# Two seven-product down-projections of a streaming-encoder trunk: their first four products interleaved instead of half after half

## What is computed

```python
for i in range(DEPTH):                      # DEPTH = 4
    h = _rmsnorm(x, norm_mix[i])
    ...                                     # y = mixer of this layer
    x = x + y
    x = x + jnp.square(jax.nn.relu(_rmsnorm(x, norm_mlp[i]) @ mlp_w1[i])) @ mlp_w2[i]
return _rmsnorm(x, norm_final)              # mlp_w1: 1024 x 4096, mlp_w2: 4096 x 1024
```

## Time and profile before

| what | value |
|---|---|
| median of three runs | 2018.82 us |
| the profiled execution: its own time | 2018.45 us |
| the profiled execution: first to last instruction | 2016.7 us |
| granted TensorE clock over the span | 0.999 of full speed |
| TensorE / VectorE / ScalarE / GpSimd busy | 98% / 78% / 55% / 17% |
| share of the chain that ended last | TensorE 84%, VectorE 11%, ScalarE 3% |
| eight stretches from the first down product of slice 1 or 2 to the next up product | 360.61 us, 45.05 or 45.12 each |

### The profile page before, as it was taken

The page is one execution under the profiler, slowest core; times in us unless marked ns, Lnnn a source line. Parts: engine busy times, 40 slices in busy tenths (PEclk is TensorE's granted clock), DMA queues, the critical chain, the costliest instruction groups (busy, mean ns, idle before and its releaser), DMA issues.

```text
span 2016.7 us, 31611 instructions
## 1 busy us (share of the span) xinstructions
PE 1975.1 (98%) x12912; PEld 1779.3 (88%) x12912; DVE 1572.5 (78%) x1898; ACT 1100.7 (55%) x1540; POOL 346.7 (17%) x403
## 2 busy tenths in 40 slices
PE   9999999999999999999999999999999999999998
PEld 7888899999878889999888889999988888899997
DVE  7866878885898878887598786888687758688874
ACT  6655534545466645455456663554647646354463
POOL 7002001110200201113731201111731011011100
PEclk9999999999999999999999999999999999999999
DMA  6122457765222266667332145685632123468761
GB/s 192 63 67 72 140 136 167 194 141 162 89 85 91 87 157 157 159 155 184 119 88 71 58 151 139 165 205 141 169 86 71 57 69 126 110 166 189 173 189 42
DMA packets 232352, 256.31 MB, mean 127 GB/s; under 512 B 19632, under 2 KB 191216, under 8 KB 232208
## 3 DMA queue, kind: packets, MB, share of 16 engines
q1 hardware_dynamic: 183024, 207.01, 32.2%
q0 software_dynamic: 46784, 45.89, 14.6%
q10 hardware_dynamic: 2400, 1.38, 0.2%
HBM read 248.21 MB, written 2.10 MB: 124 GB/s over the span
## 4 chain that ended last, share of the span: by engine, by line
PE 84%; DVE 11%; ACT 3%; issue 2%; DMA 0%; SPq 0%; DVEq 0%; ACTq 0%
PE psum L772 26%; PE psum L774 25%; PE psum L773 25%; DVE w_lo L1611 2%; PE psum L1245 2%; DVE u_lo L1844 1%; ACT w_hi L2663 1%; DVE arena_r L1844 1%; DVE x L1901 1%; PE psum L1218 1%; DVE arena L1850 1%; PE psum L1353 1%; DVE h_lo L1638 1%; PE psum L1194 1%; PE psum L1190 1%
## 5 line engine op out<-in xcount | busy, mean ns | idle before, releaser
L1611 DVE TENSOR_TENSOR w_lo<-w_raw,w_hi 128x1024 fp32r<-128x1024 f32 x339 | 415.1, 1232 | 193.7 <-ACT w_hi L2663 192.3
L2663 ACT ACTIVATE w_hi<-w_raw 128x1024 fp32r<-128x1024 f32 x343 | 358.4, 1058 | 367.3 <-PE psum L774 237.4
L772 PE MATMUL psum<-u_hi,w_hi 128*128 128x512 f32 (+1 forms) x1256 | 439.9, 350 | 12.0 <-DVE u_lo L1844 7.4
L772 PE MATMUL psum<-h_hi,w_hi 128*128 128x256 f32 (+1 forms) x1368 | 440.6, 322 | 1.1 <-DVE w_lo L1611 1.1
L773 PE MATMUL psum<-h_lo,w_hi 128*128 128x256 f32 (+1 forms) x1368 | 437.3, 320 | 0.0
L774 PE MATMUL psum<-h_hi,w_lo 128*128 128x256 f32 (+1 forms) x1368 | 437.3, 320 | 0.0
L774 PE MATMUL psum<-u_hi,w_lo 128*128 128x512 f32 (+1 forms) x1256 | 433.9, 345 | 0.0
L773 PE MATMUL psum<-u_lo,w_hi 128*128 128x512 f32 (+1 forms) x1128 | 398.4, 353 | 0.0
L773 PE MATMUL psum<-arena_r,w_hi 128*128 128x256 f32 x1184 | 331.8, 280 | 0.0
L772 PEld LDWEIGHTS psum<-h_hi,w_hi 128*128 128x128 f32 x1368 | 260.1, 190 | 21.1 <-DVE w_lo L1611 1.6
L773 PEld LDWEIGHTS psum<-h_lo,w_hi 128*128 128x128 f32 x1368 | 260.4, 190 | 19.1 <-issue 1.2
(11 more groups left out here) (380 smaller groups left out, 3208.0 us busy)
## 6 DMA issues: line engine op xcount, KB each, us to landing
w_raw<-in_mlp_w SPq DMA_DIRECT2D x204, 512.0 KB, 4.9
arena<-in_mlp_w SPq DMA_DIRECT2D x92, 512.0 KB, 4.9
w_raw<-in_mlp_w POOLq DMA_DIRECT2D x52, 512.0 KB, 6.1
arena<-in_mlp_w POOLq DMA_DIRECT2D x28, 512.0 KB, 6.0
w_raw<-in_mla_w_o SPq DMA_DIRECT2D x16, 512.0 KB, 3.5
w_raw<-in_lru_w_in SPq DMA_DIRECT2D x16, 512.0 KB, 4.0
w_raw<-in_swa_w_in SPq DMA_DIRECT2D x12, 512.0 KB, 3.9
w_raw<-in_mla_w_ukv SPq DMA_DIRECT2D x8, 512.0 KB, 4.2
```

The lines of the kernel that those rows point to most:

```text
L772: nc.tensor.matmul(out, stat[0], mov[0], start=start, stop=False, skip_group_check=skip)
L1611: ins = nc.vector.tensor_tensor(w_lo[:, to], tile, exact(w_hi[:, to]), ALU.subtract)
L2663: nc.scalar.activation(w_hi[:, to], raw_tile(op.raw), ACT.Copy).then_inc(w_hi_done, 1)
```

## The change

The two `seven_down` become one `both_down`. TensorE runs `U11` for half 0 and half 1, then `UT1` for both, `U21` for both, `UT3` for both; then `UT2`, `UT4`, `U22` of half 0, and the same three of half 1. The number of products, matmuls, loads, accumulating DMAs, splits and additions is as before; only the order is new, on all five engines. The weights' order follows (`raws` and `ops` in the plan), and so do DVE's and ACT's streams. A11+A21 is now given up before the last sum instead of after it, so its slot comes free one tile earlier. The diff, cut to the functions that stand in the new order:

```diff
@@ -200,28 +200,34 @@ (weight_plan)
-    def seven_down(i, s, g):
...
+    def both_down(i, s):
+        def blocks(g):
+            return blocks_of(lambda half, n: ("w2_block", i, s * SLICE + half * T, g * T + n, BLOCK))
+        halves = blocks(0), blocks(1)
+        for order in (0, 4, 2, 3, 1):
+            raws.extend(half[order] for half in halves)
+        for a, e, b, p, q in halves:
+            ops.append(Operand("A11", a))
+            a.freed = len(ops)
+        for a, e, b, p, q in halves:
+            ops.append(Operand("A21+A22", q))
+            q.freed = len(ops)
+        for a, e, b, p, q in halves:
+            ops.append(Operand("A12", b))
+        for a, e, b, p, q in halves:
+            ops.append(Operand("A11+A21", p, (p, e)))
+        for g, (a, e, b, p, q) in enumerate(halves):
+            ops.append(Operand("A11+A21+A22", p, made=sums + 1 + g))
+            down_sums.append((b, p))
+            ops.append(Operand("A22", e))
+            p.freed = e.freed = len(ops)
+            ops.append(Operand("A11+A12+A21+A22", b, made=sums + 3 + g))
+            b.freed = len(ops)
+        sums += 4
...
-        raws.extend((a, q, b, p, e))
...
@@ -298,6 +304,7 @@
+X_FIRST, X_V, X_Y, X_Z, X_SECOND = (1, 2), (3, 5), (7, 8), (9, 10), (11, 13)
@@ -951,32 +958,35 @@ (tensor engine)
-            def seven_down(g):
...
+            def both_down():
+                c.add("downs", 2)
+                halves = (0, 1), (2, 3)
+                for g, (xy, own) in enumerate(halves):
+                    claim(xy)
+                    pe.wait_ge(u_turned, n + 1)
+                    group(bank(xy, 0), U11, False)
+                for g, (xy, own) in enumerate(halves):
+                    claim(own)
+                    pe.wait_ge(u_turned, n + 2)
+                    group(bank(own, 1), UT1, False)
+                for g, (xy, own) in enumerate(halves):
+                    pe.wait_ge(u_turned, n + 3)
+                    group(bank(xy, 1), U21, False)
+                for g, (xy, own) in enumerate(halves):
+                    pe.wait_ge(u_turned, n + 4)
+                    group(bank(own, 0), UT3, False)
+                for g, (xy, own) in enumerate(halves):
+                    pe.wait_ge(u_turned, n + 5)
+                    pe.wait_ge(x_added, 7 * d + X_FIRST[g])
+                    group(bank(xy, 0), UT2, True)
+                    pe.wait_ge(u_turned, n + 7)
+                    pe.wait_ge(x_added, 7 * d + X_Z[g])
+                    group(bank(own, 0), UT4, True)
+                    pe.wait_ge(x_added, 7 * d + X_SECOND[g] + 1)
+                    group(bank(xy, 0), U22, True)
@@ -1887,60 +1896,91 @@ (vector engine)
-            def seven_down(g, n):
...
+                def add_first(g):
+                    add(x11[g], X[g], 0).then_inc(x_added, 1)
+                def add_v(g):
+                    add(x22[g], V[g], 0, ALU.subtract).then_inc(x_added, 1)
+                    add(x12[g], V[g], 0).then_inc(x_added, 1)
+                def add_y(g):
+                    add(x11[g], Y[g], X_FIRST[g]).then_inc(x_added, 1)
+                def add_z(g):
+                    add(x22[g], Z[g], X_V[g]).then_inc(x_added, 1)
+                def add_second(g):
+                    add(x22[g], X[g], X_Z[g], ALU.subtract).then_inc(x_added, 1)
+                    add(x21[g], X[g], 0, ALU.subtract).then_inc(x_added, 1)
+                u_low(n, 3, U21)
+                dve.wait_ge(u_squared, 4 * n + 4)
+                nc.vector.tensor_tensor(kept[0][1], kept[0][1], kept[1][1], ALU.subtract).then_inc(u_turns, 1)
+                dve.wait_ge(u_high, 7 * n + 2)
+                nc.vector.tensor_tensor(minus_t1, minus_t1, kept[1][1], ALU.subtract).then_inc(u_turns, 1)
+                split(1)
                 product_passed()
+                add_first(0)
+                u_low(n, 4, UT3)
+                dve.wait_ge(u_turns, 4 * n + 3)
+                nc.vector.tensor_tensor(kept[1][0], kept[1][0], minus_t1, ALU.add).then_inc(u_turns, 1)
                 product_passed()
+                add_first(1)
+                split(1)
+                u_low(n, 5, UT2)
                 product_passed()
+                split(1)
+                add_v(0)
+                u_low(n, 6, U22)
                 product_passed()
+                split(1)
+                add_v(1)
+                u_low(n, 7, UT4)
+                product_passed()
+                split(1)
+                add_y(0)
+                product_passed()
                 add_blocks(*down_sums[d])
+                split(1)
+                add_y(1)
                 product_passed()
+                split(1)
+                add_z(0)
                 product_passed()
+                split(1)
+                add_z(1)
                 product_passed()
+                add_second(0)
+                add_blocks(*down_sums[d + 1])
+                split(1)
+                product_passed()
+                free(add(x21[0], Z[0], X_SECOND[0] + 1), 1)
+                split(1)
+                product_passed()
+                free(add(x12[0], X[0], X_V[0] + 1), 0)
+                split(1)
+                product_passed()
+                add_second(1)
+                split(1)
+                product_passed()
+                free(add(x21[1], Z[1], X_SECOND[1] + 1), 3)
+                split(1)
+                product_passed()
+                free(add(x12[1], X[1], X_V[1] + 1), 2)
+                split(1)
+                for a in range(4):
                     dve.wait_ge(area_free[a], c.now(f"area{a}"))
@@ -2894,25 +2933,21 @@ (scalar engine)
-            def seven_down(g, n):
...
+            def both_down(n):
+                split(1)
+                act.wait_ge(u_turns, 4 * n + 2)
+                u_high_of(UT3)
+                act.wait_ge(u_turns, 4 * n + 3)
+                u_high_of(UT2)
+                split(1)
+                act.wait_ge(u_squared, 4 * n + 4)
+                u_high_of(U22)
+                split(1)
+                act.wait_ge(u_turns, 4 * n + 4)
+                u_high_of(UT4)
+                c.add("tensor_unit", 14)
+                split(11)
```

106 lines of the change are left out of this document (11 added, 95 removed).

## The result

| what | before | after |
|---|---|---|
| median of twelve runs | 2018.82 us (2018.52 to 2021.20) | 2022.72 us (2019.94 to 2029.28) |
| ratio to before, 95% interval | 1 | 1.0021 [1.0011, 1.0031] |
| profiled execution: its time / span | 2018.45 / 2016.7 us | 2021.04 / 2019.2 us |
| granted TensorE clock over the span | 0.999 | 0.997 |
| the eight down-projection stretches | 360.61 us | 362.70 us |

The change makes the kernel about 4 us slower. The forecast was 2017.6; the time lies in the range of 2014.5 to 2027, but on the other side of no change than forecast. The single times are also spread wider than before: over 9 us instead of 3.

A forecast was written before the change was run, and what follows sets the result against it. TensorE's waits in eight down-projection stretches, set by VectorE's run, were taken as the bound. The stall moves: 2018.45 less 1.2 (0.15 per stretch) gives 2017.2, or 2017.6 against the median; range 2014.5 to 2027.

The forecast's parts named there:

- the bound: Eight down-projection stretches: TensorE idles 4.8 us in each, 38 us in all, the most any order can win.
- The three waits for low parts: Waits ahead of `U21`, `UT3` and `UT2` in each down-projection stretch go: with restarts about 3 us of the 4.8.
- The stall moving to the addition of z: `UT4` of half 0, the tenth product, waits for VectorE's addition of z, so the new stretch loses 4.6 us.
- The waits ahead of the eighth, ninth and tenth product: TensorE's new waits per stretch: about 0.5 and 1.7 us for splits, about 2.2 us for an addition to x.
- `U22` "just in time": Additions for `U22` of half 0 end at T + 33.3, TensorE arrives at 33.4; a miss costs 0.1 to 0.2 us.
- The gain of 0.15 us per stretch: Each down-projection stretch shortens from 45.08 to 44.93 us, 1.2 us in eight.
- One reading: Outside the eight down-projections TensorE nowhere waits for more than 1 us.
- The step that failed: From `UT4` to the stretch's end: five products at 2.88 us plus 0.06 for the restart, 14.46 us, ending at T + 44.93.
- All that can change is TensorE's idle time in the eight stretches.: Work on every engine stays the same: fourteen products, same loads, accumulating DMAs, splits and additions.
- The first rival: Second accumulating DMA lands at T + 2.3 to 3.9, late by 0.1 to 1.7 us; up to 12 us slower; chance 0.20.
- In time, 0.7 us to spare: Second accumulating DMA of the pair lands about T + 1.5, ahead of ScalarE's rounding at T + 2.2 (T: stretch's start).
- The far gain: Rival: VectorE adds z early enough, by an earlier or shorter run; up to 38 us go, 1980 us; chance 0.03.

The follow-up runs named there:

- experiment 8: Changed kernel with VectorE's order by due time and the pair of accumulating DMAs taken apart; 1984.45 us.
- experiment 5: Changed kernel with z of half 0 added one split earlier and the accumulating DMAs taken apart, 2018.13 us; also the changed kernel rerun unedited, 2021.67 us.
- two-by-two table: Changed kernel 2021.67 us; with z of half 0 added one split earlier 2018.73; with accumulating DMAs taken apart 2021.17; with both edits 2018.13.
- experiment 3: Kernel before, with VectorE splitting the weights of `U22` of half 0 one addition later; 2034.06 us, ratio 1.0075.
- experiment 4: Changed kernel with a plain load put between the two tiles with an accumulating DMA; 2021.17 us, ratio 1.0013.
- experiment 2: Changed kernel with VectorE's addition of z of half 0 one split later; 2039.65 us, ratio 1.0107.
- experiment 1: Changed kernel with VectorE's addition of z of half 0 one split earlier; 2018.73 us, ratio 0.9997.
- experiment 6: Changed kernel with the six additions of v and y moved behind the second additions of x; 1993.05 us, ratio 0.9870.
- experiment 7: Changed kernel with VectorE's order by due time, two versions: last three products interleaved too, 2003.35 us; TensorE's order kept, 1985.11 us.

## Why the prediction was wrong

*Right:* the bound (TensorE's idle time in eight stretches, 4.8 us each, 38 in all: experiment 8 won exactly that there). The three waits for low parts going. The stall moving to the addition of z, by the count of 19 long and 8 short instructions: T + 29.69 forecast, T + 29.66 measured. The waits ahead of the eighth, ninth and tenth product, 0.5, 1.7 and 2.2 forecast, 0.36, 1.55 and 2.05 measured. `U22` "just in time": no wait. The gain of 0.15 us per stretch: 44.93 forecast, 44.87 to 44.96 in the six undisturbed stretches, and 1.2 us in all once the two disturbances are taken away (experiment 5; that it agrees to a tenth is chance, its interval is 0 to 3.4 us). One reading was off without a consequence: TensorE waits for more than 1 us outside the eight stretches as well, once, 1.1 us for a split ahead of the first of them.

*The step that failed* is the one behind `UT4`: "Then five products, with the slow first matmul of a restart: 5 x 2.88 + 0.06 = 14.46", and above it the sentence "All that can change is TensorE's idle time in the eight stretches." A product costs 2.88 us only at the full clock: in the last stretch these five products took 15.96 us, from 1909.07 to 1925.03. The restart was priced by the waits of the kernel before, none over 1.6 us, and the new order makes one of 2.05. In two of the eight stretches, in each of three profiled executions of kernels with this wait, the price was 1.4 to 1.5 us on top of the 0.06. Over the medians of the two-by-two table it is 3 us, which turns -1.2 into about +2. In the first comparison it came to +4: five of its twelve executions have a granted clock of 0.996 or less, so more falls than the two in the profiled one, but none of these was profiled.

The Trainium skill has this in "TensorE: Matmul & The Clock Gate", section "What's actually happening": a monitor sets the array's clock to one of two levels by how busy TensorE has been. The rows agree on both levels (matmuls 0.12 and 0.21 us apart). The prediction should have named it as a rival: its own numbers had the longest wait grow from 1.6 to 2.2 us.

*The first rival*, the second accumulating DMA late, was given 0.20 for 8 stretches by about 1 us. In the profiled executions ScalarE waits for it in one or two stretches, by 0.3 to 1.3 us, and the medians put 0.5 to 0.6 us on it, within the noise; the order of before is not free of it either (experiment 3). "In time, 0.7 us to spare" was right for most stretches and wrong for the tail. The Trainium skill's "DMA: Bandwidth & Descriptors", section "Queues, rings and completion order", has an engine take turns between its queues; read as equal shares, the prediction's first rival, it would have landed at T + 2.3 to T + 3.9 in every stretch. The landing at T + 2.61 lies within that, the one at T + 0.06 does not, so that reading is not borne out as a rule.

*The far gain* ("if VectorE made z's addition early enough ... 1980", chance 0.03) was not what this change does, but it was there to be had: 1984 to 1985. The prediction's argument against it, that the run has as much work as it has, took the order inside the run as given. Six of its eight additions are due later than z.

## What to carry to other kernels

Idle time of TensorE isn't all of one price: when an edit merges or lengthens waits, look at the longest single wait and not only at the sum; if it grows past what the kernel before shows, price a fall of the clock for it, and if it can't be removed, split it by moving one instruction of the engine it waits for. When a stall "moves", list what stands in the late engine's run and for whom; an operation that nobody waits for soon belongs behind the ones that are waited for. An order with later deadlines gains little until the engine that serves them uses the room: here the interleaving alone gave 1.2 us, and with VectorE's order by due time 34. Whether VectorE's order would have gained something without the interleaving was not run. By the rows it can't gain much there: of the 17 instructions between the start of VectorE's run (316.37) and the split for `U22` (333.69), none is an addition of v or y, and all serve `U22` or a product ahead of it.

## What the runs showed of the hardware

The falls of TensorE's clock by the wait right ahead of them, counted over the eight stretches of each profiled execution: with 2.05 us, 6 of 24 (the changed kernel twice, experiment 4); with 2.15 to 2.21 us, 4 of 8, and with 2.44 us, one of one (all experiment 3); with 3.2 us, 7 of 8 (experiment 2). With a longest wait of 1.5 to 1.6 us there is none in 24 (the kernel before, experiment 1, both edits of experiment 5), with about 1.0 none in 8 (experiment 6), and none in the 24 stretches of experiments 7 and 8, of which one has a wait of 1.2 us and the others next to none. In the up-projections of experiment 7 a wait of 1.9 us was followed by a fall in one place and not in another. So it is no fixed bound; why one stretch has it and the next, with the same wait, has not, stays open. The changed kernel had its falls in the same two stretches both times it was profiled, experiment 4 in another pair.

The kernel before may not be wholly free of them either, to go by its mean granted clock: in the sessions of the experiments it is 0.999 or 1.0 in 42 of 50 executions and 0.997 or 0.998 in eight, among them the three slowest (up to 2022.21 us). None of the eight was profiled, so whether its clock fell in the stretches, and behind which wait, is not shown.

One fall costs 1.4 to 1.5 us after a wait of 2.05, 1.5 to 1.7 after 2.2 and 3.2; it begins 0.3 to 1.7 us after the restart. Since their number changes from one execution to the next, they also widen the spread: 2.1 and 4.2 us over eleven executions each with a granted clock of 0.999 or more throughout (both edits of experiment 5, and experiment 1), 5.8, 9.3 and 11.6 with them (the changed kernel twice, experiment 4). The mean granted clock of an execution tells them: 0.996 to 0.998 where the changed kernel took up to 2026.98 us, 0.994 and 0.993 where it took 2027.52 and 2029.28.
